# A two-layer encoder on one core: another order of the first loads, and the first weight unit in two halves

## The reference, cut to what matters

```python
mod = silu(c) @ w_ada[l] + b_ada[l]             # 1024 -> 6 * 1024
sh1, sc1, g1, sh2, sc2, g2 = split(mod, 6)
h = rms_norm(x, norm1_g[l]) * (1 + sc1) + sh1   # rms over the 1024 channels
z = h @ w_in[l]                                 # conv, short conv, q, k, v inputs
...                                             # two convolutions, rope, differential attention
x = x + g1 * (concat(ya, yb, yc) @ w_out[l])
h = rms_norm(x, norm2_g[l]) * (1 + sc2) + sh2
x = x + g2 * ((silu(g) * u) @ w_down[l])        # g, u = split(h @ w_gate_up[l])
```

## Time and profile before

| | us |
|---|---|
| median of 3 runs | 1187.54 (1187.30 to 1188.18) |
| the profiled execution: its span, first to last instruction | 1186.5 |
| what the median has above that span | 1.04 |
| busy in the span: PE | 1175.3 |
| PEld | 929.8 |
| DVE | 728.5 |
| ACT | 506.8 |
| POOL | 119.3 |

### The profile page before, as it was taken

One profiled execution on the slowest core, in us unless ns is written; L12 is line 12 of the kernel. 1 busy time (PEld: TensorE's weight loads), 2 busy tenths in 40 slices (PEclk: granted clock), 3 DMA queues, 4 the chain that ended last, 5 costly groups with the idle time before them and its releaser, 6 DMA issues.

```text
span 1186.5 us, 14451 instructions
## 1 busy us (share of the span) xinstructions
PE 1175.3 (99%) x5168; PEld 929.8 (78%) x5168; DVE 728.5 (61%) x1056; ACT 506.8 (43%) x768; POOL 119.3 (10%) x195
## 2 busy tenths in 40 slices
PE   9999999999999999999999999999999999999998
PEld 6787556878888888888888876678888888888887
DVE  7989998985556432577478998757733333332221
ACT  5546788463222232322234468866523232332220
POOL 2321232211012000121000112100000000000000
PEclk9999999999999999999999999999999999999999
DMA  8777346986565323697323764423332323223332
GB/s 302 249 240 178 80 96 197 307 264 212 186 199 170 106 89 106 227 314 256 106 89 102 165 142 94 85 54 107 107 106 88 106 89 98 96 93 105 105 104 88
DMA packets 48940, 175.18 MB, mean 148 GB/s; under 512 B 5697, under 2 KB 5825, under 8 KB 48898
## 3 DMA queue, kind: packets, MB, share of 16 engines
q1 hardware_dynamic: 30386, 107.13, 27.7%
q0 software_dynamic: 18512, 67.51, 20.4%
HBM read 172.52 MB, written 2.10 MB: 147 GB/s over the span
## 4 chain that ended last, share of the span: by engine, by line
PE 84%; DVE 10%; ACT 4%; issue 2%; DVEq 0%; ACTq 0%; POOL 0%; POOLq 0%
PE ps L1699 22%; PE ps L1700 22%; PE ps L1701 22%; PE ps L1728 3%; DVE uc L1229 3%; PE ps L1765 2%; PE ps L1767 2%; PE ps L1766 2%; PE ps L1732 2%; ACT prob L783 1%; PE ps L1970 1%; DVE neg_max L1333 1%; PE ps L1747 1%; PE ps L1755 1%; PE ps L1748 1%
## 5 line engine op out<-in xcount | busy, mean ns | idle before, releaser
L644 ACT ACTIVATE w_hi<-raw 128x1024 fp32r<-128x1024 f32 x196 | 207.5, 1060 | 519.7 <-PE ps L1701 465.7
L1041 DVE TENSOR_TENSOR w_lo<-raw,w_hi 128x1024 fp32r<-128x1024 f32 x164 | 201.5, 1228 | 240.6 <-ACT w_hi L644 238.5
L1699 PE MATMUL ps<-h_hi,w_hi 128*128 128x512 f32 x832 | 329.0, 395 | 0.0
L1701 PE MATMUL ps<-h_lo,w_hi 128*128 128x512 f32 x832 | 324.1, 390 | 0.0
L1700 PE MATMUL ps<-h_hi,w_lo 128*128 128x512 f32 x832 | 324.1, 389 | 0.0
L1699 PEld LDWEIGHTS ps<-h_hi,w_hi 128*128 128x128 f32 x832 | 156.2, 188 | 48.5 <-issue 17.3
L1701 PEld LDWEIGHTS ps<-h_lo,w_hi 128*128 128x128 f32 x832 | 156.2, 188 | 32.8
L1700 PEld LDWEIGHTS ps<-h_hi,w_lo 128*128 128x128 f32 x832 | 156.3, 188 | 31.2 <-issue 0.5
L1699 PE MATMUL ps<-gu_hi,w_hi 128*128 128x512 f32 x352 | 136.9, 389 | 0.0
L1700 PE MATMUL ps<-gu_hi,w_lo 128*128 128x512 f32 x352 | 136.9, 389 | 0.0
L1701 PE MATMUL ps<-gu_lo,w_hi 128*128 128x512 f32 x352 | 136.9, 389 | 0.0
(11 more groups left out here) (225 smaller groups left out, 1408.9 us busy)
## 6 DMA issues: line engine op xcount, KB each, us to landing
raw<-w_stream SPq DMA_DIRECT2D x196, 512.0 KB, 3.4
w_lo<-w_stream POOLq DMA_DIRECT2D x32, 512.0 KB, 7.9
ada_ring_gu<-ada POOLq DMA_DIRECT2D x28, 512.0 KB, 4.3
ada_ring_late<-ada POOLq DMA_DIRECT2D x28, 512.0 KB, 5.0
ada_ring_first<-ada POOLq DMA_DIRECT2D x16, 512.0 KB, 5.0
ada_ring_mid_a<-ada POOLq DMA_DIRECT2D x12, 512.0 KB, 5.0
ada_ring_mid_b<-ada POOLq DMA_DIRECT2D x12, 512.0 KB, 4.9
xT<-x_t SPq DMA_DIRECT2D x4, 512.0 KB, 5.6
```

Source lines behind the costliest of these rows:

```text
L644: act.activation(w_hi[:, u % RING, :], raw[:, u % RAW, :], ACT.Copy).then_inc(s_whi, 1)
L1041: dve.tensor_tensor(w_lo[:, u % RING, :], raw[:, u % RAW, :], w_hi[:, u % RING, :].bitcast(F32), ALU.subtract).then_inc(s_wlo, 1)
L1699: pe.matmul(dst, whi, rhs[0][:, n, :], start=start, stop=False)
L1701: return pe.matmul(dst, whi, rhs[1][:, n, :], start=False, stop=stop)
```

## The change

SP issues x first, then modulation blocks 1 and 0 (on semaphores of their own), pcol, unit 0 in two halves and unit 1 without a wait. ACT issues c, positions and frequencies, loads the silu table set itself, makes four squares, then silu of c, then the other four squares. ACT's copy of unit 0 moves behind the making of 1/rms: the first half before the first gain, the second behind the first `norm_hi`. DVE makes the low parts of the two halves around the first `norm_lo`, followed by that of unit 1 and then the dot of block 2. The first warm-up is 10 matmuls in place of 14. PE's first `a_chunk` waits for the first half alone. POOL no longer loads blocks 0 and 1; it loads 2 to 5 when 0 to 3 have landed.

```diff
--- before.py
+++ after.py
@@ -335,6 +335,9 @@
             return (wa, wb)[t // 2][:, t % 2, :]
 
         s_raw = [sem(f"raw_landed{i}") for i in range(RAW)]
+        s_rawpart = sem("first_half_unit_landed")
+        s_whipart = sem("first_half_unit_hi")
+        s_wlopart = sem("first_half_unit_lo")
         s_whi = sem("weight_hi")
         s_wlo = sem("weight_lo")
         s_nhi = sem("weight_negative_hi")
@@ -350,6 +353,7 @@
         s_const = sem("constants_set")
 
         s_ada = [sem(f"ada_landed{i}") for i in range(8)]
+        s_adafirst = [sem(f"ada_first_landed{i}") for i in range(2)]
         s_ada_gu = [sem(f"ada_gu_landed{i}") for i in range(4)]
         s_cps = sem("c_spread")
         s_cact = sem("c_act_ready")
@@ -461,9 +465,12 @@
 
             if M_GU <= m < M_DOWN:
                 eng.wait_ge(s_ada_gu[m % 4], 16 * ((m - M_GU) // 4 + 1))
+            elif m < 2:
+                eng.wait_ge(s_adafirst[m], 16)
             else:
                 before = m // 8 if m < M_GU else M_GU // 8 + (m - M_DOWN) // 8
-                eng.wait_ge(s_ada[m % 8 if m < M_GU else (m - M_DOWN) % 8], 16 * (before + 1))
+                slot = m % 8 if m < M_GU else (m - M_DOWN) % 8
+                eng.wait_ge(s_ada[slot], 16 * (before + (slot >= 2)))
 
         def chunks_before(k):
 
@@ -478,16 +485,14 @@
 
         @block.sync
         def _(sp):
-            sp.dma_start(c_row[:], c_in).then_inc(s_c, 16)
-            sp.dma_start(pos_i[:], pos_in).then_inc(s_pos, 16)
-            sp.dma_start(freq[:], freq_in.partition_broadcast(P)).then_inc(s_fr, 16)
             for i in range(KC // 2):
                 sp.dma_start(xT[:, 2 * i:2 * i + 2, :], x_in[:, 2 * i:2 * i + 2, :]).then_inc(s_x[i], 16)
+            for m in (1, 0):
+                sp.dma_start(ada_slot(m), ada_in[m]).then_inc(s_adafirst[m], 16)
             sp.dma_start(pcol[:], pcol_in).then_inc(s_pc, 16)
-            for j in range(RAW):
-                if j == 1:
-                    ada_landed(sp, 0)
-                sp.dma_start(raw[:, j, :], w_in[j]).then_inc(s_raw[j], 16)
+            sp.dma_start(raw[:, 0, 0:T], w_in[0][:, 0:T]).then_inc(s_rawpart, 16)
+            sp.dma_start(raw[:, 0, T:UE], w_in[0][:, T:UE]).then_inc(s_raw[0], 16)
+            sp.dma_start(raw[:, 1, :], w_in[1]).then_inc(s_raw[1], 16)
             begin = RAW
             for l in range(L):
 
@@ -574,13 +579,10 @@
             pool.affine_select(out=ident[:], in_=ident[:], compare_op=ALU.not_equal, fill=1.0, base=0,
                                pattern=[[-1, P]], channel_multiplier=1).then_inc(s_const, 1)
             pads()
-            pool.wait_ge(s_x[KC // 2 - 3], 16)
-            for m in range(2):
-                ada_load(m)
-            for m in range(2, 4):
+            for m in range(2, 6):
                 ada_landed(pool, m - 2)
                 ada_load(m)
-            for m in range(4, M_MID):
+            for m in range(6, M_MID):
                 pool.wait_ge(s_acc, m - 4 + 1)
                 ada_load(m)
             pool.dma_start(rows[:], rows_in.partition_broadcast(P)).then_inc(s_rw, 16)
@@ -847,15 +849,22 @@
                         src = yb[:, z - CC, :] if z < 2 * CC else oc[z % 2][:]
                     act.activation(h_hi[:, z, :], src, ACT.Copy).then_inc(s_yhi, 1)
 
-            act.wait_ge(s_cps, 1)
-            act.activation(c_b[:].rearrange("p (b t) -> p b t", b=2), ps[:, 0:2, :], ACT.Silu).then_inc(s_cact, 1)
+            act.dma_start(c_row[:], c_in).then_inc(s_c, 16)
+            act.dma_start(pos_i[:], pos_in).then_inc(s_pos, 16)
+            act.dma_start(freq[:], freq_in.partition_broadcast(P)).then_inc(s_fr, 16)
+            act.preload_act_table_set("silu_and_others")
             for k in range(KC):
+                if k == KC // 2:
+                    act.wait_ge(s_cps, 1)
+                    act.activation(c_b[:].rearrange("p (b t) -> p b t", b=2), ps[:, 0:2, :],
+                                   ACT.Silu).then_inc(s_cact, 1)
                 act.wait_ge(s_x[k // 2], 16)
                 act.activation(sq0[:, k, :], xT[:, k, :], ACT.Square).then_inc(s_sq, 1)
             act.preload_act_table_set("natural_log_exp_and_others")
             act.wait_ge(s_const, 2)
-            split_hi(0)
             norm_rstd(0)
+            act.wait_ge(s_rawpart, 16)
+            act.activation(w_hi[:, 0, 0:T], raw[:, 0, 0:T], ACT.Copy).then_inc(s_whipart, 1)
             act.wait_ge(s_pc, 16)
             act.wait_ge(s_n1b, 1)
             first_gain(0)
@@ -865,6 +874,9 @@
                 if l == 0:
                     for k in range(KC):
                         norm_hi(0, 0, k)
+                        if k == 0:
+                            unit_raw_wait(act, 0, 0, 0)
+                            act.activation(w_hi[:, 0, T:UE], raw[:, 0, T:UE], ACT.Copy).then_inc(s_whi, 1)
                         if k < RING - 1:
                             split_hi(k + 1)
                         else:
@@ -1411,9 +1423,8 @@
             dve.scalar_tensor_tensor(n1b[:], pcol[:, 0, C_BADA + 1:C_BADA + 2 * KC:2], 1.0, pcol[:, 0, C_N1:C_N1 + KC],
                                      ALU.add, ALU.mult).then_inc(s_n1b, 1)
             dve.wait_ge(s_cact, 1)
+            mod_dot(1)
             mod_dot(0)
-            mod_dot(1)
-            split_lo(0)
             dve.wait_ge(s_nrs, 1)
 
             for l in range(L):
@@ -1422,12 +1433,19 @@
                     for k in range(KC):
                         dve.wait_ge(s_gain0, 2 * k + 2)
                         norm_apply(0, 0, k)
+                        if k == 0:
+                            dve.wait_ge(s_whipart, 1)
+                            dve.tensor_tensor(w_lo[:, 0, 0:T], raw[:, 0, 0:T], w_hi[:, 0, 0:T].bitcast(F32),
+                                              ALU.subtract).then_inc(s_wlopart, 1)
                         if k and k + 1 < KC:
                             mod_dot(2 * k + 2)
                         norm_lo(0, 0, k)
                         if k == 0:
+                            dve.wait_ge(s_whi, 1)
+                            dve.tensor_tensor(w_lo[:, 0, T:UE], raw[:, 0, T:UE], w_hi[:, 0, T:UE].bitcast(F32),
+                                              ALU.subtract).then_inc(s_wlo, 1)
+                            split_lo(1)
                             mod_dot(2)
-                            split_lo(1)
                         if k + 1 < KC:
                             mod_dot(2 * k + 3)
                         if k:
@@ -1737,7 +1755,10 @@
             def a_chunk(l, u, n):
 
                 r = n % 2
-                weights_split(u)
+                if u == 0 and n == 0:
+                    pe.wait_ge(s_wlopart, 1)
+                else:
+                    weights_split(u)
                 if l:
                     pe.wait_ge(s_yghi, n + 1)
                 else:
@@ -1829,7 +1850,7 @@
             for b in range(2):
                 mm = pe.matmul(ps[:, b, :], ones[0:1, :], c_row[:, b * T:(b + 1) * T], start=True, stop=True)
             mm.then_inc(s_cps, 1)
-            warm_up(N_WARM)
+            warm_up(N_WARM - 4)
             for k in range(0, KC, 2):
                 pe.wait_ge(s_pair, k // 2 + 1)
                 mm = pe.matmul(ps[:, B_STAT, :], ones[:], sq0[:, k, :], start=k == 0, stop=k == KC - 2)
```

## The result

The changed kernel takes 1196.75 us (median of four runs, 1195.5 to 1197.65) against 1187.68 for the kernel before beside it: ratio 1.0074, 95% interval 1.0062 to 1.0086, 9.07 us. That is 0.7% slower, clear of the noise, 8.5 us above the forecast and far outside its range. The profiled execution took 1196.53 us with a span of 1194.7, 8.2 more than before.

What follows compares the result with a forecast made beforehand. PE, busy 99%, was taken as the bound, so only the stretch before its solid run counts. Terms -0.55 + 0.53 + 0.60 + 0.23 = +0.8 gave span 1187.3, plus 1.04 outside it: 1188.3 us, range 1186.5 to 1190.5.

Steps and rivals of the forecast that it cites:

- the delay of freq: Frequencies loaded from ACT while x streams: bounds 0 and 3.0 us later, 0.2 taken.
- Rival C: Small loads late at the start: freq 2.9 us later, N 17.8, W +3.1, time 1190.6; chance 0.18.
- A: Rival: PE's rate does not rise before the sum of squares; N 18.5, +3.8 in all, 1191.3; chance 0.15.
- N: Event on PE: the sum of squares is done, at 16.1 us before; forecast 15.55.
- the halves: Unit 0 split in two on ACT and DVE behind N: +0.53, +0.60 and +0.23 us on the path.
- W: Event on DVE: weight unit 3's low part is done, at 35.45 us before; forecast +0.8.
- the short warm-up: Fewer PE matmuls ahead of the sum of squares: N 0.55 us earlier, if the rate rises at about 12.4.
- x first: SP issues x 1.3 us earlier, last quarter landing at 9.3 instead of 10.6; worth nothing by itself.
- Rival D: x lands no earlier because three queues share the engines; ends at the forecast, no chance of its own.
- gives nothing: Removing ACT's copy of unit 0 before N and DVE's subtraction before the first gain: both stood ahead of waits, worth 0.
- Squares, modulation blocks and raw unit 2: Squares ending near 10.7 and earlier blocks worth nothing; later request for unit 2 taken as 0, 0.8 us kept for range.
- What W moves, the end moves: From W to the end of the kernel: any shift of W shifts the end, as PE has no idle to hide it.

Runs made afterwards that it cites:

- e5: Changed kernel with positions and frequencies loaded for 32 of the 128 partitions only, the rest zeroed by POOL; 1194.07 us, ratio 1.0051.
- e4: Changed kernel with unit 0 loaded and split whole instead of in halves; 1194.71 us, ratio 1.0069.
- e10: Kernel before with 10 warm-ups instead of 14, nothing else; 1187.98 us, ratio 1.0001.
- e6: Changed kernel with the small loads on SP ahead of x and unit 0 whole; 1188.30 us, ratio 1.0005.
- e8: e6 with the reduction of the angles also moved from DVE's chunk 1 to chunk 3; 1187.71 us, ratio 1.0001.
- e1: Changed kernel with c, positions and frequencies on SP's queue again, ahead of x; 1188.88 us, ratio 1.001.
- e7: Kernel before with the reduction of the angles moved from DVE's chunk 1 to chunk 3; 1187.60 us, ratio 0.9999.
- e3: Changed kernel with 30 warm-up matmuls in place of 10 ahead of the sum of squares; 1194.37 us, ratio 1.0058.
- e9: Changed kernel with SP waiting for c's landing before it issues x; 1190.27 us, ratio 1.002.
- e2: Kernel before with only c, positions and frequencies moved to ACT, ahead of everything; 1195.26 us, ratio 1.006.

## Why the prediction was wrong

**The step that failed** is the delay of freq: "I take 0.2, near the lower end, because the three are 22 KB". It measured 4.8 us (7.8 for 3.0), beyond even the upper bound of 3.0. Size was the wrong measure. pos and freq have 16 packets on each engine, and e5 puts 0.16 us on each, some 2.6 in all, as if each waited its turn beside a 4 KB packet of x; another 2.2 us of the delay don't go by the rows, and what they are stays open. The bound was wrong in kind: twofold spread among 512 KB loads, all of which already had company, says nothing on what company does to a small load that had little. The argument for the low end, DMA engines 9% busy while freq was under way, described the conditions that the change removed. It was also a partial reading: 9% is the window from 2 to 3 us, and freq was under way until 4.59, beside a DMA share of 0.53 from 3 to 4. Rival C, built on the packets, named the right load and about 60% of the size (2.9 for 4.9).

**A and C were priced as if they excluded each other.** The late freq is what makes the hole long. A had a hole of 0.9 us in mind; it became 5.4, long enough for the clock to fall, and the sum took 6.32 us for 3.60. C's +4.9 and A's +2.7, less the 0.95 by which PE's own warm-up had held the sum back, make N 6.7 late. Neither rival's 1191 had both. The price of A, 0.85 a matmul, was nearly right: 6.32 is 0.79 each.

**Right: the halves.** +1.36 was forecast and W - N rose by 1.31 here and by 1.32 between e4 and the changed kernel. The parts stand where they were put: the first h_hi matmul comes 4.10 after Ln for 3.58 before (+0.52), the second half at 27.48, and unit 1's subtraction 0.1 us after its end, where 0.2 was forecast.

**Right in kind, near in size by luck: the short warm-up.** "0.55 earlier", if the rate rises, against 0.38 in e10, where it rose. But e10's freq was 0.47 late, and in e6, e8 and e10 the whole sum ran at the full pace, from 11.44, 11.47 and 11.99 (3.70 us each), so the one slow matmul and the rise "at 12.4 as now" did not come; in e6 the sum is done 0.9 us earlier than before. The condition attached to the term was the one that failed, for a reason outside it. The rival's "without a hole from 6.35" is too short as well: PE had worked without a hole since 1.10.

**Wrong, at no cost here: x first.** Its last quarter was to land at 9.3. It landed at about 10.3 (up to 8.2 us from issue for 7.1), against 10.6 before, and ACT waited 0.93 us for it. Rival D, by which x lands no earlier, was nearly right on this; its reason, the shared DMA engines, no run tests. DVE was in the angles, so it did not matter.

**Right in the kernel as changed, wrong as a general statement:** removing ACT's copy from before N "gives nothing". In the kernel before it had 2.04 us of slack. With two blocks ahead of unit 0 it has none (e6), so there the halves earn back some 0.7 of their 1.3 (1.32 less the 0.6 by which e6 is below e1). Squares, modulation blocks and raw unit 2 cost nothing, as forecast: ACT waited 10 us for the sum, and no wait for unit 2 appears.

**A misreading without effect:** the 1.04 us added to the span. It took the span of one execution and the median of others. In every execution here whose span is known the time is 1.7 to 1.9 above its own span (1196.53 for 1194.7; 1188.36 for 1186.5). The forecast is in effect the median plus 0.8, and that stands.

**Half right:** "What W moves, the end moves". It holds for every loss (span - W is constant within 0.4 while W goes from 35.1 to 43.5), not for a gain: of e7's 1.4 us, 0.5 arrive in the profiled execution and 0.1 in the median. The prediction would have credited a lead in full.

## What to carry to other kernels

A load of many small rows on the critical path should be landed, or under way, before a large stream starts in another queue: 22 KB came 4.8 us late here, and the same loads ahead of x in x's own queue, or x issued 0.6 us behind them in the other, gave 7.9 and 6.5 of the 9.07 us back. Count packets for each engine, not only bytes, and don't bound a contended price by rows that had no contention, or by rows that all had it. And when a late input opens a hole on an engine whose clock can fall, price the lateness and the lower rate together; they are one case.

## What the runs showed of the hardware that was not expected

- The 16 KB of freq in 128 rows took 3.0 us with x behind it in the same queue (2.9 to 3.5 in six kernels), 3.5 with x issued 0.6 us after it in another, and 7.8 with x issued 0.95 us ahead of it in another (7.5 to 8.3 in four).
- The granted clock reads 1.00 from the start of the trace, although the first warm-ups ran at half the later pace (0.22 for 0.12 us each). In this kernel it shows the first fall, at 14.9, and the rise; before its first change the column can't be relied on.
- When the rate rises is not fixed. The warm-ups or the sum changed pace at about 9.3 us in e4, 10 in e3, by 11.5 in e6 and e8, by 12.0 in e10 and at 12.4 before, but only at 15 to 16 in the profiled executions of e1 and e9, whose sums took 5.55 and 5.47 us with holes of 0.5 and 1.1 us ahead of them, while holes of 0.45 and 0.48 us in e6 and e8, 1.0 in e10 and 1.9 in e3 preceded sums at the full rate. So among these short holes the length doesn't decide. The granted clock reads 1.00 all through e1 and e9, so it doesn't tell the two levels apart there. By the Trainium skill, "TensorE: Matmul & The Clock Gate", Part 1, the rate goes by how busy the array has been of late. That agrees with the holes of 3.8 to 5.8 us in e5, e2, the changed kernel and e4, each followed by a slow sum; what decides between e1 and e10 stays open.
- In the changed kernel, e2, e4 and e5 the recorded clock fell at 14.9, 15.7, 12.7 and 13.6 us, that is 3.9, 3.1, 2.5 and 2.9 us into the hole, and rose at 21.7, 22.5, 19.6 and 20.4. How much of the sum lay ahead of the rise tells its length: 6.32, 6.71, 5.40 and 6.65 us.
